# Summing the experts' rows on TensorE, with the residual, by diagonals of their gates

## The reference, cut to what matters

```
y = hier_moe(tokens, w_rg[l], b_rg[l], w_re[l], b_re[l], w1[l], w3[l], w2[l])
if not last:
    ctx = layer_norm(ALPHA * ctx + mod_c[5] * y[b_ * s_:].reshape(b_, c_len, d_), ln2_g[l], ln2_b[l])
x = layer_norm(ALPHA * x + g2 * y[:b_ * s_].reshape(b_, s_, d_), ln2_g[l], ln2_b[l])
```

## Time and profile before

| what | us |
|---|---|
| median of 3 runs (lowest, highest) | 2927.01 (2926.5, 2927.69) |
| the profiled execution: its time, its span | 2924.71, 2922.9 |
| PE busy in the span | 2574.4 (88%) |
| DVE busy | 1359.9 (47%) |
| ACT busy | 606.6 (21%) |
| POOL busy | 588.2 (20%) |
| mean granted clock of PE | 0.937 of full speed |

### The profile page before, as it was taken

One profiled execution on the slowest core, in us unless ns is written; L12 is line 12 of the kernel. 1 busy time (PEld: TensorE's weight loads), 2 busy tenths in 40 slices (PEclk: granted clock), 3 DMA queues, 4 the chain that ended last, 5 costly groups with the idle time before them and its releaser, 6 DMA issues. The chain is left out here.

```text
span 2922.9 us, 45624 instructions
## 1 busy us (share of the span) xinstructions
PE 2574.4 (88%) x17041; PEld 1732.0 (59%) x17042; DVE 1359.9 (47%) x2657; ACT 606.6 (21%) x1315; POOL 588.2 (20%) x596
## 2 busy tenths in 40 slices
PE   7999999999999998998988999898779885798764
PEld 6877856578886474556655555454458663454332
DVE  6752357337998962245544222222244644232223
ACT  3540158321000011105432000000030722000001
POOL 3432112004441001220202300000113022222101
PEclk9999999999999999998998999999989997899887
DMA  4232311119544743003026889999750316899996
GB/s 146 94 109 83 141 73 30 62 58 253 200 172 176 287 169 113 14 1 152 1 80 276 358 357 411 413 413 396 295 195 1 152 57 274 355 367 390 394 419 245
DMA packets 141486, 597.90 MB, mean 205 GB/s; under 512 B 22705, under 2 KB 43470, under 8 KB 94770
## 3 DMA queue, kind: packets, MB, share of 16 engines
q1 hardware_dynamic: 90290, 361.46, 32.7%
q10 hardware_dynamic: 42384, 213.80, 18.3%
q0 software_dynamic: 8688, 21.00, 2.0%
HBM read 577.26 MB, written 33.75 MB: 209 GB/s over the span
## 5 line engine op out<-in xcount | busy, mean ns | idle before, releaser
L1440 DVE SCALAR_TENSOR_TENSOR psum<-weight_ring,condition_rows 128x1024 f32<-128x1024 f32 x192 | 268.1, 1396 | 16.0 <-issue 0.9
L268 PE MATMUL psum<-weight_ring 128*128 128x256 f32 (+1 forms) x896 | 221.5, 397 | 3.3 <-POOL weight_ring L253 3.3
L3034 PE MATMUL psum<-weight_ring,residual 128*32 128x256 f32 x2176 | 143.1, 408 | 77.2 <-DMA weight_ring<-in_w_dram 47.8
L3023 PE MATMUL psum<-weight_ring,residual 128*64 128x256 f32 x1792 | 205.8, 383 | 0.5 <-issue 0.5
L268 PEld LDWEIGHTS psum<-weight_ring 128*128 128x128 f32 x896 | 170.4, 190 | 43.3 <-issue 4.6
L3023 PEld LDWEIGHTS psum<-weight_ring,residual 128*64 128x64 f32 x1792 | 127.5, 138 | 76.6 <-issue 17.2
L174 PE MATMUL psum<-ffn_hidden,weight_ring 128*128 128x512 f32 (+1 forms) x440 | 154.4, 514 | 4.1 <-DVE ffn_hidden L1485 4.1
L2967 POOL DMA_INDIRECT residual<-token_rows,gather_index x87 | 95.8, 1102 | 293.5 <-issue 276.0
L3034 PEld LDWEIGHTS psum<-weight_ring,residual 128*32 128x32 f32 x2176 | 72.9, 116 | 131.9 <-issue 97.6
L3023 PE MATMUL psum<-third_stream_weights,residual 128*64 128x256 f32 x896 | 114.6, 414 | 37.8 <-DMA third_stream_weights<-in_w_dram 37.7
L174 PEld LDWEIGHTS psum<-ffn_hidden,weight_ring 128*128 128x128 f32 x440 | 84.6, 192 | 73.8 <-issue 69.3
(11 more groups left out here) (538 smaller groups left out, 4674.7 us busy)
## 6 DMA issues: line engine op xcount, KB each, us to landing
third_stream_weights<-in_w_dram ACTq DMA_DIRECT2D x93, 2048.0 KB, 14.4
weight_ring<-in_w_dram SPq DMA_DIRECT2D x84, 2048.0 KB, 17.5
weight_ring<-in_w_ada_dram SPq DMA_DIRECT2D x24, 2048.0 KB, 8.4
weight_ring<-in_w_ffn_dram SPq DMA_DIRECT2D x11, 2048.0 KB, 12.4
weight_ring<-in_w_rnn_dram SPq DMA_DIRECT2D x8, 1536.0 KB, 6.6
weight_ring<-in_w_att_dram SPq DMA_DIRECT2D x6, 2048.0 KB, 8.1
weight_ring<-in_w_in_dram SPq DMA_DIRECT2D x6, 2048.0 KB, 8.8
weight_ring<-in_w_down_dram SPq DMA_DIRECT2D x8, 1408.0 KB, 6.1
```

What stands on the lines that cost most here:

```text
L268: last = c.nc.tensor.matmul(to, weights[:, k * P:(k + 1) * P], rhs[:, k], start=(starts and k == 0), stop=(stops and k == KH - 1), skip_gr ...
L1440: last = v.scalar_tensor_tensor(out=product, in0=w[:, t], scalar=1.0, in1=CR[:, n, :], op0=ALU.mult, op1=ALU.mult, accum_out=c.mod[:, i // ...
L3023: last = nc.tensor.matmul(ps[units.rows(o), 2 + b, 256 * m:256 * (m + 1)], XT[:, b, k % tiles, units.rows(k // tiles)], w[:, k, 256 * o:25 ...
L3034: last = nc.tensor.matmul(ps[units.rows(2 * m + o), 2 + b, 0:256], XT[:, b, k % tiles, units.rows(k // tiles)], w[:, k, 256 * o:256 * (o + ...
```

## The change

The experts' rows are summed on PE. DVE builds, for each tile and choice, a 128x128 diagonal matrix of the gates. PE adds three products per half of the row in PSUM: the identity by XR(i), and each diagonal by its gathered rows. The statistics and the normalising read this sum from PSUM, and the normalised rows go to XR(i). Sums take PSUM banks 0 to 3, two banks by turns; turned tiles take banks 4 to 7, so there is now one set for all pairs. Ten products that nothing reads stand at the front of PE's list, and the three of L3340 are gone. PE's order is add(0), add(1), then for each i add(i + 2) and turn(i). ACT and DVE write four column tiles of every pair each, after tile 2p + 3 is normalised, and the copies follow. The last tile is normalised half by ACT and half by DVE.

```diff
--- before.py
+++ after.py
@@ -3270,18 +3270,19 @@
 
 
     nc, ps, X, ring = c.nc, c.ps, c.X, c.ring
-    WIDTH, per = 256, 2
+    WIDTH, per, warm = 256, 2, 10
     npair = nt // per
     rows_in = [c.sig(f"combine_rows_landed{i}") for i in range(nt)]
     summed, turned, stats_ready = c.sig("combine_done"), c.sig("rows_turned"), c.sig("ln_stats_ready")
     rooted, scaled, normalised = c.ph[1:]
+    diagonals, half_normalised = c.sig("gate_diagonals_ready"), c.ph[0]
     out_act, out_dve, copied = c.sig("combine_out_act"), c.sig("combine_out_dve"), c.sig("combine_residual_out")
     with ExitStack() as ctx:
         def sb(name, shape):
             return ctx.enter_context(nc.sbuf_tensor(f"{name}_{l}", shape, F32))
 
         BN, MV, ROOT = sb("ln2_bn", [P, TT, 2, 6]), sb("ln2_mean_var", [P, TT, 2]), sb("ln2_root", [P, TT + 1])
-        SC = sb("ln2_scale", [P, TT, 2])
+        SC, DIAG = sb("ln2_scale", [P, TT, 2]), sb("gate_diagonals", [P, TT, 2, P])
         held = 2 * nt // 4
         spare_row = lambda r: ring.view(ring.uses - 1 - r // 4)[:, (r % 4) * D:(r % 4 + 1) * D]
         choice = lambda k, i: spare_row(2 * i + k)
@@ -3289,9 +3290,10 @@
             ring.used(summed.sem, summed.base + nt, n=ring.uses - 1 - n)
         cols = lambda p: slice(p * WIDTH, (p + 1) * WIDTH)
         group = lambda p: 0 if p * WIDTH < S else 1
-        turned_at = lambda p, k: ps[:, 4 * (p % 2) + k // 2, (k % 2) * WIDTH:(k % 2 + 1) * WIDTH]
-        whole = lambda p, h: ps[:, 4 * (p % 2) + 2 * h:4 * (p % 2) + 2 * h + 2, :].rearrange("p a (k t) -> p (a k) t", k=2)
-        last_pair = npair - 1
+        sum_of = lambda i: ps[:, 2 * (i % 2):2 * (i % 2) + 2, :]
+        turned_at = lambda p, k: ps[:, 4 + k // 2, (k % 2) * WIDTH:(k % 2 + 1) * WIDTH]
+        whole = lambda p, h: ps[:, 4 + 2 * h:4 + 2 * h + 2, :].rearrange("p a (k t) -> p (a k) t", k=2)
+        halves = lambda x: x.rearrange("p (h n) -> p h n", h=2)
         if modulated:
             HX, to = modulated
             out_of = lambda p, k: (HX[:, k, cols(p)], c.mod[:, to, 8 + k, group(p):group(p) + 1],
@@ -3316,67 +3318,83 @@
                 if store:
                     for p in range(npair):
                         out_act.wait(sp, p + 1)
-                        if p == last_pair:
-                            out_dve.wait(sp, 1)
+                        out_dve.wait(sp, p + 1)
                         sp.dma_start(c.ios["outT"].rearrange("(k p) t -> p k t", p=P)[:, :, cols(p)],
                                      X[:, :, cols(p)]).then_inc(store.sem, 16)
                     store.wait(sp, 16 * npair)
 
             @block.tensor
             def _(pe):
-                for i in range(nt):
+                def add(i):
+                    rows_in[i].wait(pe, 32)
+                    diagonals.wait(pe, i + 1)
+                    if i >= 2:
+                        normalised.wait(pe, i - 1)
+                    for h in range(2):
+                        part = slice(h * D // 2, (h + 1) * D // 2)
+                        out = ps[:, 2 * (i % 2) + h, :]
+                        nc.tensor.matmul(out, c.ident[:, :], XR(i)[:, part], start=True, stop=False)
+                        for k in range(2):
+                            last = nc.tensor.matmul(out, DIAG[:, i, k, :], choice(k, i)[:, part], start=False, stop=(k == 1))
+                    last.then_inc(summed.sem, 1)
+
+                def turn(i):
                     p = i // per
                     normalised.wait(pe, i + 1)
-                    if p >= 2 and i % per == 0:
-                        out_act.wait(pe, p - 1)
-                        copied.wait(pe, sum(q <= p - 2 for q in copies))
+                    if i == nt - 1:
+                        half_normalised.wait(pe, 1)
+                    if p >= 1 and i % per == 0:
+                        out_act.wait(pe, p)
+                        out_dve.wait(pe, p)
+                        copied.wait(pe, sum(q < p for q in copies))
                     for k in range(KT):
                         at = (i % per) * P
                         last = nc.tensor.transpose(turned_at(p, k)[:, at:at + P], XR(i)[:, k * P:(k + 1) * P], c.ident[:, :])
                     last.then_inc(turned.sem, 1)
-                    if i == nt - 2:
-                        for n in range(3):
-                            rest = ps[:, 4 * (p % 2) + n, :].rearrange("p (k t) -> p k t", k=2)[:, :, P:]
-                            nc.tensor.matmul(rest, c.ident[:, :], XR(0)[:, 0:WIDTH], start=True, stop=True)
+
+                for n in range(warm):
+                    nc.tensor.matmul(ps[:, 4 + n % 4, :], c.ident[:, :], XR(0)[:, 0:512], start=True, stop=True)
+                add(0)
+                add(1)
+                for i in range(nt):
+                    if i + 2 < nt:
+                        add(i + 2)
+                    turn(i)
 
             @block.scalar
             def _(act):
                 a = nc.scalar
 
-                def write(p, tiles):
-                    for k in tiles:
+                def write(p):
+                    turned.wait(act, per * p + per)
+                    for k in range(KH):
                         to_, scale, shift = out_of(p, k)
                         last = a.activation(to_, turned_at(p, k), ACT.Identity, scale=scale, bias=shift)
-                    return last
-
-                def copy(p, h):
-                    return a.copy(X[:, h * KH:(h + 1) * KH, cols(p)], whole(p, h))
+                    last.then_inc(out_act.sem, 1)
+
+                def copy(p):
+                    for h in range(2):
+                        if h == 1:
+                            out_dve.wait(act, p + 1)
+                        last = a.copy(X[:, h * KH:(h + 1) * KH, cols(p)], whole(p, h))
+                    last.then_inc(copied.sem, 1)
 
                 a.activation(ROOT[:, TT:TT + 1], c.eps, ACT.Sqrt)
                 for i in range(nt):
                     stats_ready.wait(act, i + 1)
                     a.activation(ROOT[:, i:i + 1], MV[:, i, 1:2], ACT.Sqrt, bias=c.eps).then_inc(rooted.sem, 1)
                     p = i // per - 1
-                    for h in range(2):
-                        if p >= 0 and i % per == 0:
-                            if h == 0:
-                                turned.wait(act, per * p + per)
-                            last = write(p, range(h * KH, (h + 1) * KH))
-                            if h == 1:
-                                last.then_inc(out_act.sem, 1)
-                        if p in copies and i % per == 1:
-                            last = copy(p, h)
-                            if h == 1:
-                                last.then_inc(copied.sem, 1)
-                        if h == 0:
-                            scaled.wait(act, i + 1)
-                            a.activation(XR(i), XR(i), ACT.Identity, scale=SC[:, i, 0:1], bias=SC[:, i, 1:2])\
-                                .then_inc(normalised.sem, 1)
-                turned.wait(act, nt)
-                write(last_pair, range(KH)).then_inc(out_act.sem, 1)
-                if last_pair in copies:
-                    copy(last_pair, 0)
-                    copy(last_pair, 1)
+                    scaled.wait(act, i + 1)
+                    part = slice(0, 1 if i == nt - 1 else 2)
+                    a.activation(halves(XR(i))[:, part], sum_of(i)[:, part], ACT.Identity,
+                                 scale=SC[:, i, 0:1], bias=SC[:, i, 1:2]).then_inc(normalised.sem, 1)
+                    if p >= 0 and i % per == 1:
+                        write(p)
+                        if p in copies:
+                            copy(p)
+                write(npair - 1)
+                if npair - 1 in copies:
+                    copy(npair - 1)
 
             @block.vector
             def _(dve):
@@ -3389,35 +3407,39 @@
                     v.scalar_tensor_tensor(out=SC[:, i, 1:2], in0=MV[:, i, 0:1], scalar=-1.0, in1=SC[:, i, 0:1],
                                            op0=ALU.mult, op1=ALU.mult).then_inc(scaled.sem, 1)
 
-                def add(k, i):
-                    return v.scalar_tensor_tensor(out=XR(i), in0=choice(k, i), scalar=R.gate[:, k, i:i + 1], in1=XR(i),
-                                                  op0=ALU.mult, op1=ALU.add)
+                def write(p):
+                    turned.wait(dve, per * p + per)
+                    for k in range(KH, KT):
+                        to_, scale, shift = out_of(p, k)
+                        last = v.tensor_scalar(to_, turned_at(p, k), scale, shift, ALU.mult, ALU.add)
+                    last.then_inc(out_dve.sem, 1)
 
                 for i in range(nt):
-                    rows_in[i].wait(dve, 32)
-                    add(0, i)
-                    if i >= 1:
-                        finish(i - 1)
-                    dve.drain()
-                    add(1, i).then_inc(summed.sem, 1)
-                    dve.drain()
+                    for k in range(2):
```

(27 more changed lines are left out.)

## The result

The changed kernel takes 2958.06 us (median of 4 runs, 2953.93 to 2959.75), the kernel before beside it 2926.76 (4 runs, 2924.15 to 2927.69): a ratio of 1.0104, 95% interval 1.0092 to 1.0115. It is slower by 31.3 us; 2959 was predicted. The profiled execution after took 2953.93, its span is 2952.1. PE is now busy 2645.0 us instead of 2574.4, DVE 1346.1 instead of 1359.9.

The account below looks back on a forecast made before the run. DVE's sums were taken to bound both combines, and PE to be slower at them. 18.4 (layer 0) + 1.6 (next stage) + 12.4 (layer 1) = +32.4 us on 2924.71, plus 2.3 for the median: 2959, range 2948 to 2967.

Parts of the forecast that it names:

- The three stretches: Layer 0's combine, the next stage's first products and layer 1's combine: predicted to grow by 18.4, 1.6 and 12.4 us.
- A product is two records, a tile 5.17 us: PE's float32 sums in both combines: 0.86 us per 512-column product, 12 records of 0.431 us a tile.
- rival of one column per cycle: PE's sums: a product takes 0.21 us, 1.3 a tile, so the kernel is not slower, 2922.5 us; chance 4%.
- Fillers 10.3 us, for full clock: Ten unread products ahead of each combine's first sum: 8.62 us plus 1.7 for cold start, buying full clock for the sums.
- rival of a clock that stays low: Both combines: the fillers don't lift PE's clock, a tile's sums take 10.3 us, total 3027 us; chance 3%.
- Statistics from PSUM cost as from SBUF: DVE's statistics of the sums: 686 ns from either memory, so reading PSUM adds nothing.
- Diagonals hidden: DVE's building of 12 or 8 matrices: at most 8.2 us for 12, covered by landing rows and fillers.
- turn(2) stalls: Layer 0 on PE: turn(2) waits 1.6 us until pair 0 is written and copied from the single bank set.
- Tails: From the last sum to the last write: 13.3 us in layer 0, 11.2 in layer 1, with cold last turns.
- Next stage cold: The stage after layer 0's combine starts at PE's lower clock: +1.6 us, bounds 0 and 2.95.
- No load late, nothing absorbed: Next stage: weight loads cost no wait; the rival that it absorbs layer 0's delay gave 2939.4 us, chance 3%.
- The signs: Timeline marks: fillers end near 2116 and 2897, next stage's first product near 2166, last write near 2930.

Follow-up runs that it names:

- e1: The changed kernel without its ten unread products at the front of PE's list: 2957.82 us, ratio 1.0094 to the kernel before.
- e3: The changed kernel with sums, statistics and normalising back on DVE and SBUF, and no unread products: 2936.76 us, ratio 1.0030 to the kernel before.
- e4: The changed kernel with turn(i) ahead of add(i + 2), and writes and copy moved ahead of the normalise: 2953.04 us, ratio 1.0087 to the kernel before.
- e6: The changed kernel with 6 more unread products in PE's idle time before the last turns and 2 behind them: 2954.73 us, ratio 1.0098 to the kernel before.
- e2: The changed kernel without the identity's product by the residual rows, so the output lacks the residual: 2967.68 us, ratio 1.0137 to the kernel before.

## Why the prediction was right

The three stretches grew by 17.16 + 3.04 + 11.47 = 31.7 us; predicted were 18.4 + 1.6 + 12.4 = 32.4. The rest of the program took 2.5 us less in this execution, and so its span grew by 29.2: it was 3.55 ahead at layer 0's combine, in code that the change doesn't touch, and lost 1.1 between the combines. Step by step:

- *A product is two records, a tile 5.17 us:* right, 5.16 in the chain. The sums of three tiles, up to turn(0), ended 25.7 us after layer 0's first instruction, predicted 2131.9 - 2106.15 = 25.75. The rival of one column per cycle falls by these rows. The price that the Trainium skill gives in "VectorE: DVE Perf Modes", section "The TRN2 errata", without naming a type, 0.216 us for 512 columns, does not hold for float32 here: a product took two records of 0.43 us each.
- *Fillers 10.3 us, for full clock:* right, 10.36 and 10.32, and 1.00 in all sums, against the rival of a clock that stays low. e1 shows that they gain nothing in sum.
- *Statistics from PSUM cost as from SBUF:* right, 1.30 us for two where SBUF's took 1.29. A normalise of 1024 columns on ACT took 1.20 us; 1.25 was taken. The extra fixed cost for PSUM that the same section of the Trainium skill gives VectorE does not show in the statistics. It is not so for every DVE instruction: the half normalise of 512 columns took 0.81 us from PSUM, and 0.55 from SBUF in e3. In the changed kernel it was done ahead of the last turn, which needs it; in e4 PE stood idle for 1.00 us until it was done.
- *Diagonals hidden:* right; DVE has twelve of them done in 2.4 us under the fillers. (The bound of 8.2 us from layer 0's first instruction ends at 2114.4, not 2114.7; nothing hangs on it.)
- *turn(2) stalls:* right in place and releaser, 1.37 us instead of 1.6. Two copies take 1.94, not 2.08.
- *Tails:* 12.6 and 10.5 us instead of 13.3 and 11.2. The 16 cold turns take 3.65 and 3.43, not 3.94, the copy is shorter, and a write starts 0.67 us into the 0.78 of the half normalise.
- *Next stage cold:* the place was right, the size not: 3.04 us instead of 1.6, above even the upper bound of 2.95. Its 6.2 cold us lie near the 5.9 of the earlier trace rows, not near the 3.1 of layer 0's own row, which I had taken as the nearest. e6 shows that this term is the clock.
- *No load late, nothing absorbed:* right; the only wait of L1856 is the 2.33 us that it had before, and in e6, whose last sum is later still, its 96 records take 24.45 us.
- *The signs:* their times are on the clock of the kernel before. Layer 0 began 3.55 us earlier and layer 1 17.74 us later here, so that the fillers' ends, 2113.0 and 2915.16, stand for 2116.6 and 2897.4 (2116 and 2897 were named), the next stage's first product for 2164.6 (2166) and the last write for 2929.4 (2930).

The mechanism held; that the total came within 1 us of 2959 is luck. The two combines were put 1.2 and 0.9 us too long (0.7 of each in the tails) and the next stage 1.4 too short, which nearly cancelled, and the four executions after spread over 5.8 us.

Of the 31 us, e3 assigns some 20 to the sums' move with the fillers, and some 11 to order, banks and late writes, which no run separates. e4 and e6, with the sums on PE, take 9.6 and 3.8 us off the stretches; what they remove overlaps, the cold clock of the tail above all.

## What to carry to other kernels

Before work moves to an idle engine, price it there from a row of the same type: float32 products of 512 columns came as two records of 0.43 us, and six of them were slower than two additions on the engine that bounded. Look for the engine's share rather than for a swap: the gain came only when both engines summed, and when the steps behind the last sum were put in order (the kernel before with nothing but a reordered tail was not run). Where PE idles just ahead of a dense stage, unread products in that gap were worth 3 us in the stage behind.

## What the runs showed of the hardware that was not expected

- The time that PE stays at the lower level after it begins to work is not one number: 3.1 and 3.0 us under the fillers of after (from 0.61 over 4.0 and 0.59 over 3.7 us), over 6 under the same fillers in e6, 6.0 and 3.4 in e1, 6.2 in after's next stage. What decides it stays open.
- The level can fall while PE works: in e2 it was 1.00 in 2137 to 2140, in which PE waited most of the time, and 0.50 from 2140 to 2143, in which it was busy throughout. In e4 the next stage began behind the same 2.33 idle us as in the kernel before, but the clock was at 0.73 in its first 2.5 us and at 0.50 in the next 2, where the kernel before had 1.00 (2147.4 to 2150), and it took 26.14 us, not 24.45.
